# One core, one layer of a hybrid backbone: the low halves of split weights on VectorE, modulation rows as transposed products, and a recurrent branch pipelined by one turn

## The reference, cut to what matters

```python
m_lat = split(silu(c) @ w_mod + b_mod, 6)          # six modulation rows of D
hx = modulate(rmsnorm(x), m_lat[0], m_lat[1])      # hc: the same for the context
q, k, v, lx, lg, bg, cg, u, gates = split_cols(hx @ w_in)
att = attention(q, k, v)                           # 16 heads, 4 kv heads, 512 keys
lru = rglru(dwconv(lx), both directions) * gelu(lg)
sc  = bg * dwconv(cg * u)
y = g0 * (att @ w_o_attn) + g1 * (lru @ w_o_lru) + g2 * (sc @ w_o_sc)
x = x + m_lat[2] * (y @ w_out)
hx = modulate(rmsnorm(x), m_lat[3], m_lat[4])
x = x + m_lat[5] * peer_ffn(hx)                    # 8 heads x 16 experts for each token
```

## Time and profile before

| | |
|---|---|
| median of 3 runs | 3575.17 us (3575.26, 3572.12, 3575.17) |
| span of the profiled execution | 3572.6 us |
| busy: TensorE, its weight loads | 2841.5, 2093.1 us |
| busy: VectorE, ScalarE, GpSimd | 2281.9, 960.9, 1740.4 us |
| HBM traffic, mean | 253 GB/s |

### The profile page before, as it was taken

One profiled execution on the slowest core, in us unless ns is written; L12 is line 12 of the kernel. 1 busy time (PEld: TensorE's weight loads), 2 busy tenths in 40 slices (PEclk: granted clock), 3 DMA queues, 4 the chain that ended last, 5 costly groups with the idle time before them and its releaser, 6 DMA issues.

```text
span 3572.6 us, 43685 instructions
## 1 busy us (share of the span) xinstructions
PE 2841.5 (80%) x15344; PEld 2093.1 (59%) x15344; DVE 2281.9 (64%) x2628; ACT 960.9 (27%) x1306; POOL 1740.4 (49%) x948
## 2 busy tenths in 40 slices
PE   8878677598988889999988882877776778686677
PEld 3557566498966689999988871434342434242233
DVE  2377777788065588999989347555555555555542
ACT  1255354343145444333333320111111111011100
POOL 0133424277433267778767626544444444444442
PEclk9988888799989999999989995999998999899999
DMA  7522212365222256565556549999998999899997
GB/s 300 207 88 70 88 65 84 116 227 220 100 89 71 78 216 246 215 233 219 220 220 234 206 147 378 411 381 411 386 415 350 417 393 393 356 389 391 385 422 301
DMA packets 126150, 905.57 MB, mean 253 GB/s; under 512 B 14000, under 2 KB 15216, under 8 KB 16368
## 3 DMA queue, kind: packets, MB, share of 16 engines
q0 software_dynamic: 73728, 536.90, 36.6%
q1 hardware_dynamic: 38304, 278.94, 21.7%
q10 hardware_dynamic: 14032, 88.72, 6.3%
HBM read 900.28 MB, written 4.23 MB: 253 GB/s over the span
## 4 chain that ended last, share of the span: by engine, by line
PE 31%; DVE 30%; DMA 20%; issue 11%; ACT 4%; POOL 2%; DVEq 1%; ACTq 0%; POOLq 0%
PE ps L413 13%; DVE macc L1189 12%; DMA u<-in_peer_u,idx 11%; DMA v<-in_peer_v,idx 7%; PE ps L687 6%; PE ps L442 3%; PE ps L662 2%; DVE u L1428 2%; DVE aa L1146 1%; POOL u L1496 1%; PE ps L471 1%; PE ps L427 1%; PE ps L429 1%; PE ps L428 1%; PE ps L588 1%
## 5 line engine op out<-in xcount | busy, mean ns | idle before, releaser
L1482 POOL TENSOR_TENSOR wl<-w,wh 128x1024 fp32r<-128x1024 f32 x432 | 1102.3, 2563 | 983.0 <-ACT wh L732 982.1
L687 PE MATMUL ps<-v,dg 128*128 128x512 f32 x2048 | 945.9, 616 | 314.6 <-ACT dg L1016 164.3
L1428 DVE SCALAR_TENSOR_TENSOR u<-u,hN 128x2048 f32<-128x2048 f32 x256 | 583.2, 2291 | 496.5 <-DMA u<-in_peer_u,idx 496.3
L687 PEld LDWEIGHTS ps<-v,dg 128*128 128x128 f32 x2048 | 390.6, 196 | 865.5 <-issue 698.0
L413 PE MATMUL ps<-hx_hi,wh 128*128 128x256 f32 x2368 | 700.8, 296 | 2.9 <-DVE y L1206 1.7
L732 ACT ACTIVATE wh<-w 128x1024 fp32r<-128x1024 f32 x432 | 453.8, 1057 | 854.5 <-PE ps L413 578.7
L413 PE MATMUL ps<-hx_lo,wh 128*128 128x256 f32 x2368 | 681.5, 288 | 0.0
L413 PE MATMUL ps<-hx_hi,wl 128*128 128x256 f32 x2368 | 680.7, 287 | 0.0
L1189 DVE SCALAR_TENSOR_TENSOR macc<-mr,sT,macc 128x256 f32<-128x256 f32 x480 | 652.1, 1358 | 27.0 <-DMA mr<-in_wmod 10.2
L1496 POOL DMA_INDIRECT u<-in_peer_u,idx x256 | 329.5, 1287 | 696.3 <-DVE u L1428 535.9
L413 PEld LDWEIGHTS ps<-hx_hi,wh 128*128 128x128 f32 x2368 | 468.0, 198 | 11.4 <-issue 9.2
(11 more groups left out here) (231 smaller groups left out, 3231.8 us busy)
## 6 DMA issues: line engine op xcount, KB each, us to landing
w<-in_stream SPq DMA_DIRECT2D x264, 1024.0 KB, 4.8
mr<-in_wmod ACTq DMA_DIRECT2D x64, 1024.0 KB, 5.6
wg<-in_gates ACTq DMA_DIRECT2D x8, 512.0 KB, 3.4
u<-in_peer_u,idx POOLq DMA_INDIRECT x256, 16.4
v<-in_peer_v,idx POOLq DMA_INDIRECT x256, 17.7
xs<-in_ctx ACTq DMA_DIRECT2D x1, 2048.0 KB, 17.4
xs<-in_x ACTq DMA_DIRECT2D x1, 2048.0 KB, 23.7
x<-in_x ACTq DMA_DIRECT2D x1, 2048.0 KB, 7.5
```

The source lines that it names most:

```text
L687: last = mm(ps[:, b, :], dg[:, k % 4, :], V[n % NV][:, b * 512:(b + 1) * 512], start=(k == 0), stop=(k == TOPK - 1))
L1428: stt(U[n % NU][:, :], U[n % NU][:, :], 1.0, hN[:, t, :], ALU.mult, ALU.mult, accum_out=dot[:, t, k:k + 1])\
L1482: sub = lambda out_, a, b: nc.gpsimd.tensor_tensor(out_, a, b, ALU.subtract)
```

## The change

1. **The low halves go to VectorE.** A helper `low` there does what GpSimd's loop did, the same subtraction of 128x1024 numbers, and is called 432 times by hand between VectorE's other steps. GpSimd keeps no arithmetic.
2. **Modulation rows as transposed products.** `w_mod` is laid out transposed on the host: row n of a [128, 2048] tile is one output column's 2048 weights. `silu(c)` is broadcast to all partitions once (`srow`, made after attention), and one `scalar_tensor_tensor` with an accumulated sum (`product`) makes 128 outputs. There are 64 such tiles of 1024 KB, all in OUT1 (4 in a turn) and SC (4 in a turn), loaded on GpSimd's queue, each as soon as the product before in its buffer is done. One transpose after SC turns the 64 columns into rows, one addition and one store finish them. `chunk_sum`, `chunk_load` and `chunk_store` are gone, with TensorE's wait in them.
3. **LRU by one turn.** The projection of `lx` for turn j + 1 stands between the two sets of gate products of turn j, and the taps of turn j + 1 stand among VectorE's steps of turn j.

```diff
@@ TensorE
-            with pe.Fori(0, NCH) as j:
+            for p in range(4):
+                pe.wait_ge(*VH.at(0, f"lo_x{(p + 1) * PIECE - 1}"))
+                proj(LRU0, 0, 0, lambda blk, i: (blk, i * T), (hc, hx), part=(p,))
+            def lru_turn(j, more):
...
-                pe.wait_ge(*AL.at(j - 1, "pad1"))
-                for p in range(4):
-                    pe.wait_ge(*VH.at(0, f"lo_x{(p + 1) * PIECE - 1}"))
-                    proj(LRU0, j, 0, lambda blk, i: (blk, i * T), (hc, hx), part=(p,))
                 pe.wait_ge(*VL.at(j - 1, "gl"))
-                proj(LRU0, j, 4, lambda blk, i: (2, blk * T), (hx,), part=(0, 1, 2))
+                proj(LRU0, j, 4, lambda blk, i: (2, blk * T), (hx,))
                 pe.wait_ge(wg_in, j * 16 + 16)
                 gate_products(0)
-                proj(LRU0, j, 4, lambda blk, i: (2, blk * T), (hx,), part=(3,))
+                if more:
+                    pe.wait_ge(*AD.at(j, "pad1"))
+                    proj(LRU0, j, 8, lambda blk, i: (blk, i * T), (hc, hx))
                 gate_products(1)
...
-                    chunk_sum(j + (0, NCH, 3 * NCH)[n])
@@ ScalarE, a turn of LRU
-                for p in (5, 6, 7):
+                for p in (8, 9, 10):
                     split(LRU0, j, 8, p)
...
                 fn(gp[:, :], ps[:, 2, :], ACT.Square).then_inc(*AL.inc("gq"))
+                split(LRU0, j, 8, 11)
+                gate_work(0)
                 act.wait_ge(*VL.at(j, "gx"))
                 fn(gp[:, :], gp[:, :], ACT.Sigmoid, scale=GELU_S).then_inc(*AL.inc("gs"))
+                if more:
+                    for p in (12, 13, 14):
+                        split(LRU0, j, 8, p)
+                    pads(j + 1, j * 8 + (2 * LRU0 + 12))
+                    split(LRU0, j, 8, 15)
                 gate_work(1)
@@ ScalarE, after attention
+            act.dma_start(srow[:, :], a_crow.to_broadcast([P, D])).then_inc(crow_in, 16)
+            act.dma_start(brow[0:MT, :], a_bmod).then_inc(brow_in, 16)
+            act.wait_ge(crow_in, 16)
+            fn(ssig[:, :], srow[:, :], ACT.Sigmoid).then_inc(*AC.inc("sig"))
@@ VectorE
+            def low(first, turn, per, p):
+                s, q = (p // 2) % RING, p % 2
+                dve.wait_ge(hi_done, turn * per + (2 * (first - LRU0) + p + 1))
+                tt(wl[p % SPLITS][:, :, :], W[s][:, q * PIECE:(q + 1) * PIECE, :], wh[p % SPLITS][:, :, :].bitcast(F32), ALU.subtract)\
+                    .then_inc(lo_done, 1)
...
+            def product(i, q):
+                dve.wait_ge(mr_in[q], i * 16 + 16)
+                stt(mr[q][:, :], mr[q][:, :], 1.0, srow[:, :], ALU.mult, ALU.mult, accum_out=mcols[:, bass.ds(i * 2 + q, 1)])\
+                    .then_inc(*VC.inc(f"p{q}"))
...
             def out_section(n, h0):
                 with dve.Fori(0, NCH) as j:
-                    chunk_products(j + (0, NCH, 3 * NCH)[n])
+                    for p in range(5, 9):
+                        low(h0, j, 8, p)
+                        if n == 1:
+                            product(j * 2 + (p - 5) // 2, (p - 5) % 2)
+                    for p in range(9, 12):
+                        low(h0, j, 8, p)
...
             dve.wait_ge(rows_in, 64)
-            with dve.Fori(0, NCH // 2) as i:
+            def out_rows(i, more):
                 for c in (0, 1):
+                    for p in (range(5, 8), range(8, 12))[c] if more or c == 0 else ():
+                        low(WO0, i, 8, p)
@@ GpSimd
-            with pool.Fori(0, (WQ0 - LRU0) // RING) as i:
-                for p in range(2 * RING):
-                    pool.wait_ge(hi_done, i * (2 * RING) + p + 1)
-                    sub(wl[p % SPLITS][:, :, :], W[p // 2][:, (p % 2) * PIECE:(p % 2 + 1) * PIECE, :], wh[p % SPLITS][:, :, :].bitcast(F32))\
-                        .then_inc(lo_done, 1)
+            pool.wait_ge(*VQ.at(KVH - 1, "al11"))
+            with pool.Fori(0, MT // 2) as i:
+                for q in (0, 1):
+                    pool.wait_ge(*VC.at(i - 1, f"p{q}"))
+                    pool.dma_start(mr[q][:, :], a_wmod[bass.ds(i * 2 + q, 1)].rearrange("o p k -> (o p) k")).then_inc(mr_in[q], 16)
```

More of the change, by code:

```diff
@@ L182, in build @@
         zt = sb("zt", R_E + 2048, [P, 2 * T])
[L183 to L186, removed]
+        mr = [sb(f"mr{i}", R_E + 4096 + i * 8192, [P, D]) for i in range(2)]
+        srow = sb("srow", R_HC + 16384, [P, D])
+        ssig = sb("ssig", R_HC + 24576, [P, D])
+        brow = sb("brow", R_D + 1216, [P, P])
+        mrows = sb("mrows", R_D + 1728, [P, P])
+        mcols = sb("mcols", R_D + 2240, [P, MT])
         kT = sb("kT", R_E, [P, KVH, 2 * T])
@@ L745, in _, with pads @@
             split(LRU0, 0, 0, AHEAD - 1)
+            split(LRU0, 0, 0, 5)
+            split(LRU0, 0, 0, 6)
+            def pads(j, used):
+                act.wait_ge(piece_used, used)
+                for b in (0, 1):
+                    act.wait_ge(*VT.at(j - 1, f"tap{b}3"))
+                    fn(pad[:, b, :, LRU_TAPS // 2:LRU_TAPS // 2 + T], ps[:, b, :].rearrange("p (s t) -> p s t", s=2), ACT.Copy)\
+                        .then_inc(*AD.inc(f"pad{b}"))
+            pads(0, 2 * LRU0 + 4)
+            split(LRU0, 0, 0, 7)
             def lru_turn(j, more):
@@ new lines, in lru_turn @@
+            def lru_turn(j, more):
+                low(LRU0, j, 8, 11)
+                driven(j, 0)
+                decays(j, 0)
+                gelu_inner(j)
+                drives(j, 0)
+                if more:
+                    low(LRU0, j, 8, 12)
+                scans(j, 0)
+                if more:
+                    low(LRU0, j, 8, 13)
+                lru_out(j, 0)
+                if more:
+                    low(LRU0, j, 8, 14)
+                    taps(j + 1, 0)
+                    low(LRU0, j, 8, 15)
+                driven(j, 1)
+                if more:
+                    taps(j + 1, 1)
+                decays(j, 1)
+                if more:
+                    low(LRU0, j, 8, 16)
+                drives(j, 1)
+                if more:
+                    low(LRU0, j, 8, 17)
+                scans(j, 1)
+                low(LRU0, j, 8, 18 if more else 12)
+                lru_out(j, 1)
@@ L1303, in _ @@
             attention_turn(KVH - 1, False)
-            dve.wait_ge(*VQ.at(KVH - 1, "al11"))
+            low(OUT1, 0, 0, 4)
+            dve.wait_ge(crow_in, 16)
+            dve.wait_ge(*AC.at(0, "sig"))
+            tt(srow[:, :], srow[:, :], ssig[:, :], ALU.mult).then_inc(*VY.inc("s"))
+            dve.wait_ge(*VY.at(0, "s"))
             out_section(1, OUT1)
@@ L1354, in _ @@
                         tt(xv, xv, xm[:, :], ALU.add).then_inc(*VW.inc(f"a{c}{t}"))
+                if more:
+                    low(WO0, i, 8, 12)
+            with dve.Fori(0, NCH // 2 - 1) as i:
+                out_rows(i, True)
+            out_rows(NCH // 2 - 1, False)
             stt(gfr[:, :], m4r[:, :], 1.0, gfr[:, :], ALU.add, ALU.mult).then_inc(*VF.inc("g1"))
```

278 lines of the change are left out of this document (134 added, 144 removed).

## The result

The changed kernel took 3286.7 us in the median of 4 runs (3282.62 to 3296.09), the kernel before 3573.64 in 4 runs beside it: a ratio of 0.92, 95% interval [0.9186, 0.9214]. The profiled execution was the slowest of the four: 3296.09 us with a span of 3294.3, 9 us above the median.

A forecast was written before the change was run, and what follows sets the result against it. VectorE's sharing with GpSimd was taken to keep TensorE waiting; stage terms -135 - 41 - 31 + 3 + 5 - 26 - 31 + 7 = -249 took 3572.6 to 3323.6, plus 2.6 around the span: 3326 us, range 3290 to 3395.

The forecast's parts named there:

- the turn of LRU: In LRU: 44.5 us a turn, bound narrowly by VectorE; LRU and the start together -135 us.
- low end: Whole kernel: LRU at TensorE's 42.2 us a turn, attention at -10, L under 6.4: 3286 us, taken as 3290.
- The start and the ends of LRU: In LRU: first turn 65 us, last 32, and +3 for low halves in the chain that makes `hx`.
- OUT0, OUT2, SC, the norms, WO and routing: Terms by stage: OUT0 -41, OUT2 -31, SC -31, norms of keys +3, WO +7, routing and experts 0 us.
- the stop: In WO: TensorE stands for 17 us while VectorE waits for the rows ahead of further low halves.
- Attention: In attention: 24 low halves, 29 us, mostly covered on VectorE; +5 us, bounds -10 and +29.
- OUT1: In OUT1: VectorE waits for a load once a turn; turn 24.3 us, plus 3 for `srow`; -26 us.
- L: In OUT1: time from a product's end to the landing of its buffer's next load, taken as 7.5 us.
- Late loads: Rival, OUT1 and SC: L of 10 gives +26 us, 3352; 16.4 gives +129, 3455; chance 0.13.
- The LRU turn that stays near 52: Rival, LRU: a low half waiting for a split behind a table load delays scans; +60 us, 3386; chance 0.15.
- The slower case: Rival, VectorE: low halves cost over 1.22 us; gain gone at 2.27, some 3816 us at 3.04; chance 0.02.
- sign of being wrong: In LRU turns over 50 us, or waits of products over 5 us, would show the forecast wrong.

The follow-up runs named there:

- four buffers: The changed kernel with four buffers mr instead of two for the rows of w_mod, each used once a turn: 3284.99 us, ratio 0.9185.
- part 1 alone: The changed kernel with the old chunks back and LRU not pipelined, so that only the low halves move to VectorE: 3370.99 us, ratio 0.9427.

## Why the prediction was off

**The term that failed is the turn of LRU.** 44.5 us was 39.6 of VectorE's work, 3 of gaps and 2 of one wait. Measured are 38.5, 2.1 and 0.7, 41.3 together. To a busy time of 29.8 us I added eight low halves at their full 1.22, but each overlaps its neighbours by 0.08 us. The wait for the square root was 1.86 us in either half of a turn before, shared or not; in the new order it is left in one half and is 0.69, with the taps of the next turn ahead of it. Over six turns this is 19 us. The mechanism stands: VectorE bounds the turn, level with TensorE and not 2 us above it. What I wrote as TensorE's bound and low end, 42.2, was high too, since a gate set takes 3.44 us and not 3.71, and 96 matmuls 11.50 (23.02 for 192): it is 41.4. Had I taken this, the low end would have been some 5 us lower. Even so, the low end that I worked out was 3286, which holds the measured 3286.7; I took 3290 and gave no reason.

**The start and the ends of LRU** gave 11 us more. I had the first projection start 3 us later, for four low halves in the chain that makes `hx`; it began 3 us earlier (148.4 us, 151.1 before). What I had left out is that the sharing stretched this chain too. Before, two of its steps on `xT` ahead of TensorE's start, 0.32 us each in the chain elsewhere, took 2.37 and 2.35 us beside GpSimd's low halves; in their place one low half on VectorE adds 1.1. First and last turn together are 92 us (340.5 from the first gate projection at 174.2 us to the end of the last `br_lo`, less six turns of 41.4), forecast 97.

**Right within 5 us:** OUT0, OUT2, SC, the norms, WO and routing. WO's 3 for 7 is luck in part: the stop was forecast as 17 us and was 9, and the one before, which I had not seen, was 6. The low half (1.222 us for 1.22), the product (2.288 for 2.29), the end of sharing in all sections, full clock in OUT2 and SC are as forecast. Attention was +5 and came out at -1, within its bounds of -10 and +29: with 24 low halves, 29 us, more, VectorE's busy time rose by 13 only. How the rest divides between work that was hidden and sharing that went, no run tells. The misses of OUT0, the norms and OUT1 (+13) and those of attention, WO, SC and routing (-13) cancel, which is luck, so that LRU's 30 us are nearly the whole difference in span; the other 9 us to the median are the profiled execution's distance from it.

**OUT1** was -26 and came to -19. L was sized well (8.2 for 7.5). Left out were a second wait in the same turn, for the second buffer at 10.5 us, and the true price of `srow`: 5.6 us with four buffers, not 3. The waits come in the first turns and once near the end; from 1122.57 us on TensorE runs 96.8 us without one. The rule of the Trainium skill (DMA: Bandwidth & Descriptors, "Anatomy of one DMA — SWDGE (gpsimd) path"), an estimated 4.4 us for a load, lies below all 64 of them (4.9 to 10.3, median 5.4). By it every turn of OUT1 would have been TensorE's, and the first ones were not.

**The rivals.** Late loads with L of 10: half true, in a few turns of OUT1 only. The LRU turn that stays near 52: no, 41.4; it is 52.0 without the pipelining and 51.3 with the low halves on GpSimd, so both parts are needed. The slower case: no, the low half costs 1.22 in every section. The exclusive lock of the Trainium skill (SBUF — State Buffer, "SBUF: two separate sides"), by which the sharing ends with GpSimd's arithmetic, is borne out twice: no VectorE instruction of 3.3 us is left in LRU, and with the low halves back on GpSimd VectorE's busy time in a turn rises from 38.5 to 46.2 us with less to do.

**Of what would show it,** as listed: low halves of 1.22 us, yes; LRU turns of 44 to 45, no, 41.4; OUT0 and OUT2 at 23.2, yes; one wait for `mr` a turn, no, two or none; one stop in WO, yes, of 9 us and not 17. Neither sign of being wrong appeared: the longest wait of a product was 3.9 us.

## What to carry to other kernels

Moving 524 us of work from GpSimd to a VectorE that already looked like the busier of the two made VectorE's own busy time fall by 215 us (part 1 alone): where the same instruction shows two durations in the two halves of a turn, cost the move with the shorter one; look for the long one in every stage, also in short instructions of the start; and ask which other stalls are symptoms of it before curing them one by one. For an engine that bounds a loop narrowly, read the time from start to start of neighbours and not their durations, and test the bound from both sides (work doubled on one engine, work cut on the other): a busy share of 100% on TensorE did not make it the only bound. A wait put into an engine's order delays all that stands behind it, as the low halves behind `srow` and behind the rows of WO; low halves that others need belong ahead of it.
